# Spreading the reciprocal roots of the head norms over the partitions: one fp32 product per head, or one single-pass product of a split value

## The reference

```python
def rmsnorm(x, g):
    x32 = x.astype(F32)
    y = x32 * lax.rsqrt(jnp.mean(x32 * x32, axis=-1, keepdims=True) + EPS)
    return (y * g.astype(F32)).astype(x.dtype)
...
    q = rope(rmsnorm(qa.reshape(nb, t, A_HEADS, A_HEAD_DIM), g_aq), pos)
    k_new = rope(rmsnorm(ka.reshape(nb, t, A_KV_HEADS, A_HEAD_DIM), g_ak), pos)
...
    qn = rmsnorm(qb[..., :B_NOPE], g_qn)
    qr = rope(rmsnorm(qb[..., B_NOPE:], g_qr), pos)
...
    kn_all = rmsnorm(kvb[..., :B_NOPE], g_kn)
```

## Time and profile before

| | |
|---|---|
| median of 3 runs | 2916.06 us (2915.59 to 2917.22) |
| the profiled execution, its own time | 2909.76 us |
| its span, first to last instruction | 2908.0 us |
| PE busy | 2885.5 us, 99% of the span |
| DVE busy | 1431.8 us, 49% |
| ACT busy | 1069.1 us, 37% |
| POOL busy | 178.9 us, 6% |
| mean granted TensorE clock | 0.996 of full |

### The profile page before, as it was taken

The page is one execution under the profiler, slowest core; times in us unless marked ns, Lnnn a source line. Parts: engine busy times, 40 slices in busy tenths (PEclk is TensorE's granted clock), DMA queues, the critical chain, the costliest instruction groups (busy, mean ns, idle before and its releaser), DMA issues.

```text
span 2908.0 us, 45168 instructions
## 1 busy us (share of the span) xinstructions
PE 2885.5 (99%) x18756; PEld 2827.2 (97%) x18756; DVE 1431.8 (49%) x1518; ACT 1069.1 (37%) x1231; POOL 178.9 (6%) x103
## 2 busy tenths in 40 slices
PE   9999899999999999999999999999999999999999
PEld 9997689999999999999999999899999999999999
DVE  7677553644443344334375774446443443443443
ACT  5333432433233233233244642434333333333332
POOL 0000001200000000000130251112000000000000
PEclk9999999999999999999999999999999999999999
DMA  6433004444444444444444444344444444444443
GB/s 229 135 106 116 23 30 145 139 144 142 141 142 143 143 144 139 145 140 143 145 145 153 146 157 144 117 145 145 152 152 148 150 152 148 150 152 150 148 152 132
DMA packets 112351, 405.32 MB, mean 139 GB/s; under 512 B 12608, under 2 KB 14192, under 8 KB 112048
## 3 DMA queue, kind: packets, MB, share of 16 engines
q1 hardware_dynamic: 108864, 392.64, 40.8%
q0 software_dynamic: 1616, 6.31, 0.6%
q10 hardware_dynamic: 1696, 3.73, 0.3%
HBM read 396.54 MB, written 6.09 MB: 138 GB/s over the span
## 4 chain that ended last, share of the span: by engine, by line
PE 97%; DVE 2%; ACT 1%; issue 0%; DMA 0%; ACTq 0%; DVEq 0%
PE PS L1308 30%; PE PS L1310 30%; PE PS L1309 30%; PE PS L1398 1%; PE PS L1434 1%; PE PS L1613 0%; PE PS L1614 0%; PE PS L1384 0%; ACT pr L453 0%; PE PS L1590 0%; DVE pr L858 0%; PE PS L1381 0%; PE PS L1742 0%; PE PS L1365 0%; DVE w_lo L788 0%
## 5 line engine op out<-in xcount | busy, mean ns | idle before, releaser
L788 DVE TENSOR_TENSOR w_lo<-stage,w_hi 128x1024 fp32r<-128x1024 f32 x740 | 927.0, 1255 | 1202.6 <-ACT w_hi L405 1202.2
L405 ACT ACTIVATE w_hi<-stage 128x1024 fp32r<-128x1024 f32 x740 | 783.5, 1059 | 1643.2 <-PE PS L1310 1638.5
L1308 PE MATMUL PS<-xh,w_hi 128*128 128x336 f32 (+1 forms) x3264 | 1027.1, 315 | 1.0 <-DVE kk L1009 0.6
L1310 PE MATMUL PS<-xh,w_lo 128*128 128x336 f32 (+1 forms) x3264 | 1021.9, 313 | 0.0
L1309 PE MATMUL PS<-xl,w_hi 128*128 128x336 f32 (+1 forms) x3264 | 1020.3, 313 | 0.0
L1308 PE MATMUL PS<-hh,w_hi 128*128 128x336 f32 (+1 forms) x2048 | 640.6, 313 | 0.0
L1310 PE MATMUL PS<-hh,w_lo 128*128 128x336 f32 (+1 forms) x2048 | 640.0, 312 | 0.0
L1309 PE MATMUL PS<-hl,w_hi 128*128 128x336 f32 (+1 forms) x2048 | 639.1, 312 | 0.0
L1308 PEld LDWEIGHTS PS<-xh,w_hi 128*128 128x128 f32 x3264 | 612.9, 188 | 4.6 <-issue 1.6
L1309 PEld LDWEIGHTS PS<-xl,w_hi 128*128 128x128 f32 x3264 | 615.4, 189 | 1.1
L1310 PEld LDWEIGHTS PS<-xh,w_lo 128*128 128x128 f32 x3264 | 612.7, 188 | 0.0
(11 more groups left out here) (310 smaller groups left out, 1516.3 us busy)
## 6 DMA issues: line engine op xcount, KB each, us to landing
stage<-in_wstream SPq DMA_DIRECT2D x740, 512.0 KB, 3.3
out_y<-x ACTq DMA_DIRECT2D x4, 672.0 KB, 3.4
out_s<-so POOLq DMA_DIRECT2D x8, 256.0 KB, 2.6
x<-in_x_in SPq DMA_DIRECT2D x6, 336.0 KB, 7.1
dmask<-in_ret POOLq DMA_DIRECT2D x4, 352.0 KB, 4.7
stage<-in_wstream SPq DMA_DIRECT2D x4, 256.0 KB, 3.8
s<-in_s_in POOLq DMA_DIRECT2D x1, 1024.0 KB, 5.1
x<-in_x_in SPq DMA_DIRECT2D x4, 168.0 KB, 4.0
```

The source lines that it names most:

```text
L405: act.activation(w_hi[:, s, :], stage[:, s, :], ACT.Copy).then_inc(hi_ready, 1)
L788: dve.tensor_tensor(w_lo[:, s, :], stage[:, s, :], w_hi[:, s, :].bitcast(F32), ALU.subtract).then_inc(lo_ready, 1)
L1308: pe.matmul(out, wh, rh, start=first, stop=False)
L1310: mm = pe.matmul(out, wl, rh, start=False, stop=last)
```

## The change

DVE no longer only takes the reciprocal. `inverse_split` takes the reciprocal, writes its rounded part into rows 0 and up of a new tile `rhl` (fp32r), and what is left of it into rows 32 and up. The three operations are linked by the semaphore of DVE's own chain. A spread is then one fp32r product over the first 64 rows of `rhl`; its weights, `one_row`, hold the identity's column twice, in rows 0 to 31 and in rows 32 to 63, so that both parts are added up. `pairrow` becomes fp32r and is doubled in the same way. POOL clears `rhl` once and builds `one_row` and `pairrow` with ten copies of 32 rows where it made four of 16 rows; DVE, not PE, now waits for them (`pair_ready`), in front of the first split.

```diff
-        pairrow = place("pairrow", [P, 4, P], V + 16384)
+        pairrow = place("pairrow", [P, 4, P], V + 16384, F32R)
+        rhl = place("rhl", [P, KEYS], V + 18432, F32R)
+        one_row = place("one_row", [P, 16], V + 18432 + KEYS * 4, F32R)
...
-                        dve.reciprocal(sdq[0:16], sdq[0:16]).then_inc(qb_rinv, 1)
+                        inverse_split(sdq, 16, T, qb_rinv)
...
+            def inverse_split(sd, rows, cols, done):
+
+                ch.link(dve.reciprocal(sd[0:rows, 0:cols], sd[0:rows, 0:cols]))
+                ch.link(dve.tensor_copy(rhl[0:rows, 0:cols], sd[0:rows, 0:cols]))
+                dve.tensor_tensor(rhl[32:32 + rows, 0:cols], sd[0:rows, 0:cols], rhl[0:rows, 0:cols].bitcast(F32),
+                                  ALU.subtract).then_inc(done, 1)
...
                         dve.wait_ge(k_sd, 1)
-                        dve.reciprocal(sdr[0:8], sdr[0:8]).then_inc(k_rinv, 1)
+                        dve.wait_ge(pair_ready, 1)
+                        inverse_split(sdr, 8, T, k_rinv)
...
-                    dve.reciprocal(sdr[0:8], sdr[0:8]).then_inc(qa_rinv, 1)
+                    inverse_split(sdr, 8, T, qa_rinv)
...
-            dve.reciprocal(sdk[0:8], sdk[0:8]).then_inc(kn_rinv, 1)
+            inverse_split(sdk, 8, KEYS, kn_rinv)
...
-            def spread(out, j, rows, n=8):
-
-                return pe.matmul(out, ident[0:n, j:j + 1].to_broadcast([n, P]), rows, start=True, stop=True)
+            def spread(out, j, cols):
+
+                return pe.matmul(out, one_row[0:64, j:j + 1].to_broadcast([64, P]), rhl[0:64, 0:cols], start=True,
+                                 stop=True)
...
-                        mm = pe.matmul(PS[:, 4 + j, 0:T], pairrow[0:16, j], sdq[0:16], start=True, stop=True)
+                        mm = pe.matmul(PS[:, 4 + j, 0:T], pairrow[0:64, j], rhl[0:64, 0:T], start=True, stop=True)
...
+            pool.memset(rhl[:].bitcast(F32), 0.0).then_inc(pad_zero, 1)
             pool.wait_ge(const_in, 32)
-            for j in range(4):
-                pair = ident[0:16, 8 + 2 * j:10 + 2 * j].unsqueeze(1).unsqueeze(3).to_broadcast([16, 2, 2, 32])
-                e = pool.tensor_copy(pairrow[0:16, j].rearrange("p (r e f) -> p r e f", r=2, e=2), pair)
+            pool.wait_ge(pad_zero, 2)
+            for a in (0, 32):
+                pool.tensor_copy(one_row[a:a + 32], ident[a:a + 32, a:a + 16])
+                for j in range(4):
+                    c = a + 8 + 2 * j
+                    pair = ident[a:a + 32, c:c + 2].unsqueeze(1).unsqueeze(3).to_broadcast([32, 2, 2, 32])
+                    e = pool.tensor_copy(pairrow[a:a + 32, j].rearrange("p (r e f) -> p r e f", r=2, e=2), pair)
             e.then_inc(pair_ready, 1)
```

More of the change, by code:

```diff
@@ L1414, in hook @@
                         for j in range(3):
-                            spread(PS[:, 1 + j, 0:T], j, sdr[0:8])
+                            spread(PS[:, 1 + j, 0:T], j, T)
                         for q, (t0, _, _) in enumerate(QT):
@@ L1466, in hook @@
                         for j in range(4):
-                            mm = spread(PS[:, bank + j, 0:T], j, sdr[0:8])
+                            mm = spread(PS[:, bank + j, 0:T], j, T)
                         mm.then_inc(qa_bc, 1)
@@ L1556, in spread_qb @@
                     pe.wait_ge(qb_rinv, 1)
-                    pe.wait_ge(pair_ready, 1)
                 else:
@@ L1561, in spread_qb @@
                     if c < 2:
-                        mm = spread(PS[:, 4 + j, 0:T], 4 * c + j, sdq[0:16], 16)
+                        mm = spread(PS[:, 4 + j, 0:T], 4 * c + j, T)
                     else:
-                        mm = pe.matmul(PS[:, 4 + j, 0:T], pairrow[0:16, j], sdq[0:16], start=True, stop=True)
+                        mm = pe.matmul(PS[:, 4 + j, 0:T], pairrow[0:64, j], rhl[0:64, 0:T], start=True, stop=True)
                 mm.then_inc(qb_bc, 1)
@@ L1599, in _ @@
                 for j in range(4):
-                    mm = spread(PS[:, 4 * (1 - c) + j, 0:KEYS], 4 * c + j, sdk[0:8])
+                    mm = spread(PS[:, 4 * (1 - c) + j, 0:KEYS], 4 * c + j, KEYS)
                 mm.then_inc(kn_bc, 1)
@@ L1818, in _ @@
             pool.memset(kpad[:], 0.0).then_inc(pad_zero, 1)
+            pool.memset(rhl[:].bitcast(F32), 0.0).then_inc(pad_zero, 1)
             pool.wait_ge(const_in, 32)
-            for j in range(4):
-                pair = ident[0:16, 8 + 2 * j:10 + 2 * j].unsqueeze(1).unsqueeze(3).to_broadcast([16, 2, 2, 32])
-                e = pool.tensor_copy(pairrow[0:16, j].rearrange("p (r e f) -> p r e f", r=2, e=2), pair)
+            pool.wait_ge(pad_zero, 2)
[5 more added lines that the diff above has]
+                    e = pool.tensor_copy(pairrow[a:a + 32, j].rearrange("p (r e f) -> p r e f", r=2, e=2), pair)
             e.then_inc(pair_ready, 1)
             pool.wait_ge(k_turned, 2)
-            pool.wait_ge(pad_zero, 1)
             pool.wait_ge(past_in, 80)
```

## The result

The changed kernel takes 2898.16 us (median of 4 runs, 2896.49 to 2899.06) beside 2916.2 us for the kernel before (4 runs). The profiled execution took 2898.78 us, 11.0 us less than the profiled one of before.

What follows compares the result with a forecast made beforehand. PE bounds the kernel, busy 99% of the span and 97% of the last chain. Shorter spreads (11.05 us) and the clock (3.0 us) give 14.05 us, so 2916.06 us becomes 2902.0 us; range 2899 to 2907 us.

Steps and rivals of the forecast that it cites:

- The form of the product: Input projection: an fp32r spread of 64 rows was taken at 0.154 us, between bounds of 0.154 and 0.66 us.
- the sign: In the changed profile, the groups of spreads at g = 1, 6 and 7 should start 0.15 us apart.
- The gains at g = 1, 6 and 7: Input projection: shorter spreads save 1.33, 2.03 and 0.78 us, the last cut by PE's wait for qb.
- The waits behind the spreads: Behind attention A, PE waits for ACT's copies, qb and kn, so gains are 1.20, 0.58, 1.74 and 3.39 us.
- The seven terms: Gains of the spreads: three in the input projection and four behind attention A, 11.05 us in sum.
- What is added: DVE's two operations per place (1.1 or 1.4 us) and POOL's copies, taken as covered and counted at nothing.
- one of the prediction's own signs of being wrong: The prediction is wrong if the clock falls in keys_b(1) or values_b(0), where it should be 1.00.
- The rival that the waits hold the clock down: Falls in keys_b(1) and values_b(0) stay because PE rests there; only 11.05 us gained, 2905.0 us; chance 0.19.
- The 1.5 us for `keys_b(1)`: Behind attention A: the clock's fall in keys_b(1) was counted as gone, saving 1.5 us.
- The case at 337.77: Behind spread_qb(1), the clock fell after 2.5 us of products reading 16 rows, though PE had no idle time.
- the timed median stands 6.3 us above it and I move it by the same: From profiled execution to timed runs: 2909.76 us profiled, 2916.06 us timed, so the forecast is 2902.0 us.
- I had given the clock 3.0 us: Behind attention A: falls in keys_b(1) and values_b(0) go, 1.5 us each; those at the sums and scores stay.

Runs made afterwards that it cites:

- the DVE order: DVE does qb's two operations before sdk's reciprocal, and the late w_lo after kn's multiplications: on the changed kernel 2895.34 us, on the kernel before 2912.76 us.

## Why the prediction was right, point by point

**The form of the product.** Taken at the lower bound, 0.154 us, and nearly right. The four spreads at g = 6 start at 235.46, 235.72, 235.87 and 236.03: two of the intervals are the 0.15 us named as the sign, the first is 0.26 us. From the first spread to the next weight product it is 0.80 us for four. The stretch is 1.31 us where I had 0.93: I let the change at both ends vanish with fp32, and it stayed. The 0.38 us lie in four intervals, from the last weight product to the first spread (0.25 us), to the second spread (0.26 us), from the last spread to the weight product (0.23 us) and to the next one (0.26 us). That is the term that was mis-sized. The gains at g = 1, 6 and 7 are 2.53 - 1.44 = 1.09, 2.96 - 1.31 = 1.65 and 2.96 - 2.26 = 0.70 us; forecast were 1.33, 2.03 and 0.78.

**The waits behind the spreads.** Each came where it was put. `keys_b(1)` starts 1.49 us after the first spread and not 2.62: 1.13 us (1.20 forecast). `values_b(0)`: 333.43 to 335.30, 1.87 us and not 2.45, 0.58 us (0.58). The sums of squares: 2.67 us and not 4.32, 1.65 us (1.74). The scores: 6.50 us and not 9.79, 3.29 us (3.39). The seven terms make 10.1 us where the sum had 11.05. The two runs with the DVE order show that the last wait is DVE's chain to `kn`, as forecast: with the other order PE got 2.9 us back, and in the kernel before nothing.

**What is added.** Counted at nothing, and it costs nothing (ratio 0.9998 by itself). The copy is 0.32 us on 336 columns, and both operations take 0.9 us with their links, not 1.1. POOL's copies end at 36.27 us and not before 34; DVE asks for them so much later that nothing hangs on it.

**The clock, in the profile.** `values_b(0)` got back 7.32 - 5.80 = 1.5 us as forecast. `keys_b(1)` got nothing back in this execution (0.75 after 0.77), and the sums of squares lost 0.3 us. So 10.1 + 1.5 - 0.2 - 0.3 = 11.1 us, and the scores start 375.11 - 364.02 = 11.09 us earlier. So one of the prediction's own signs of being wrong came up: the clock fell in `keys_b(1)`, beside waits of 1.08 and 0.62 us and spreads that now read 64 rows. The rival that the waits hold the clock down was right for this place in this execution, and wrong for `values_b(0)`. The 1.5 us for `keys_b(1)` were counted as certain and are a matter of the execution: the second profile of the changed kernel has no fall there, and one of the same length ahead of it instead. The fall in `values_b(0)` was a matter of the execution too. In the second profile of the kernel before, `spread_qb(1)` is followed by this:

```profile
346.94:352.73 5.79, 5.79 (x26) 4.19 (x25) 2.84 (x2) 2.10 (x2) 0.00 (x0) 1.00 0.22 65
```

Of the five profiles whose `spread_qb(1)` is in fp32 over 16 rows, only the first has a fall in `values_b(0)`. The case at 337.77, on which the prediction rested its choice, was real but rare there.

**The step that failed** is the one from the profile to the runs: "the timed median stands 6.3 us above it and I move it by the same". The 6.3 us were no constant. They were falls of the clock that the profiled execution lacked and the timed runs had, and part of them lay behind the very spreads that the change shortens. That is why the median came out at 2898.16 us and not 2902.0, 0.8 us below the range, while the profiled execution came out at 2898.78 us and not 2895.7. The two errors have opposite signs, so that 14 us stood near the 16 us of the runs is in part luck. The ratio on record, 0.9945, would put 2916.06 us at 2900.0 us, inside the range.

**Where the gain comes from.** The run with fp32 over 64 rows splits it: 9.0 us come with the rows (2914.18 to 2905.18) and 6.9 us with the single pass (2905.18 to 2898.25). The first part is the clock, since the products are as long as before. As an estimate, lost time is span times what the mean clock lacks to 1, which for the kernel before is 2913 x 0.005 = about 15 us, and for the changed kernel 2898 x 0.002 = about 6 us (both with an uncertainty of 1.5 us from the third digit). These 9 us can't be added to the 10.1 us of shorter stages, because the 9.79 us of the eight spreads hold 3.4 us of lower clock: 10.1 + 9 - 3.4 = 15.7 us, beside 15.9 measured. Nor are the two parts of the split independent, since the single pass brings waits, and behind waits the clock still falls. I had given the clock 3.0 us. My reason for it was the right one, that the clock fell behind spreads with no rest; I applied it to one stage and not to g = 1, 6 and 7, because one execution showed no fall there.

**The page on the clock.** The Trainium skill (TensorE: Matmul & The Clock Gate, Why this matters for your kernels) has continuous work hold the clock and long idle gaps lower it. By that rule, that the waits in the spreads' place hold the clock down as the spreads did, the gain was 11 us and the time 2905.0 us. The runs decide against it for the spreads (2898.2 us): a product that reads 8 or 16 rows didn't hold the clock though PE was busy without a gap, and the same product over 64 rows did. For the rests they don't contradict it: what falls are left near these stages in the two profiles of the changed kernel lie beside waits of 0.6 to 3.25 us. Most of these waits are short, and nothing here tells whether they are the long gaps that the page means.

**What stays open.** The fall in layer 1's retention (6.8 us at the lower clock in the second profile of the kernel before, none in the first) is there in some profiles and not in others, of kernels on both sides; nothing here tells what decides it. PE waits 1.4 us for DVE ahead of it with and without the fall. It is open as well why a fall in the attention of A, such as the one at 313.96, stands in six of the nine profiles with 64 rows at g = 6 and in none of the five with 8 rows. Whether few rows would matter in an fp32r product was not tried, nor any number of rows between 16 and 64.

## What to carry to other kernels

Where one profile and the timed median of the same kernel differ by a good part of what the change is worth (here 6.3 of 14 us), look at the mean clock of several runs first; the difference may lie in the very place that is changed. When a product that covered another engine's work is made shorter, walk every wait that it hid: here three of the seven gains were cut to less than half by copies on ACT and DVE and by DVE's work ahead of `kn`, and a change of order gave back 2.9 us that the same order could not give before. A small fp32 helper product on TensorE was better off here reading 64 rows, most of them zero, than 8 or 16: it took no longer and kept the clock up.

## What the runs showed of the hardware

- Fp32 products over 8 or 16 rows, back to back and without idle time, were followed by a fall of TensorE's clock to 1.2 GHz; the same products over 64 rows, with the same length and mostly zeros, were not. Of the five profiles with 8-row spreads at g = 6, four have a fall behind them and three another behind g = 7; of the nine profiles with 64 rows there none has. Only two of these nine are fp32 and so of the same length; the mean clock of their sixteen timed runs (0.997 to 0.999, before 0.993 to 0.996) bears them out. Behind `spread_qb(0)`, 16 rows after a wait of 1.1 us, the fall comes in five profiles of five, and with 64 rows in one of nine; behind `spread_qb(1)`, 16 rows with no wait, in one of five, and with 64 rows in none. Padding alone was worth 6.9 us of 2913 us (ratio 0.9974).
- The same kernel takes 2909.7 or 2917.4 us depending on how many falls of the clock an execution meets, behind these spreads and elsewhere (mean clock 0.996 or 0.993).
- A group of four fp32r spreads of 64 rows between products of 128 rows costs 0.38 us more than the pace of 0.154 us gives, about 0.1 us at each of four intervals around its two ends. The outer two (0.25 and 0.26 us) are the same with fp32 spreads over 8 rows.
